# Two streams' memory reads in turn on two column groups of TensorE, and the first transfers of the stage in another order

## The chip, the cores and the metric

One core of one Trainium2 chip. The metric is the device time of one launch in microseconds, here the median of three runs. TensorE's granted clock is one of two levels, 1.2 or 2.4 GHz; the profile writes it as 0.5 or 1.0.

## What is computed

The whole program is one step of a two-layer streaming encoder: an S5 layer, an mLSTM layer with a matrix memory, a gated convolution FFN behind each. There are 1024 new prompt tokens and 8 running streams of 16 tokens. The change touches only the mLSTM part of the 8 running streams. Cut to that, for each of 4 heads and each of 8 streams:

```
num   = einsum('bqsh,bshd->bqhd', sc, vc) + a * einsum('bqhk,bhvk->bqhv', qc, C)   # reads of the old memory C
C_new = decay * C + einsum('blh,blhv,blhk->bhvk', wg, vc, kc)                      # update of it
```

C is a float32 matrix of 512 by 512 for each head and stream, 1 MB. So 32 memories are loaded from HBM, read, updated and stored back.

## The kernel before

`mlstm_streams` has three blocks; at the end of each, all engines meet in a barrier, and GpSimd comes to the barrier only when the transfers that it issued have landed.

The **first block** goes over the 4 heads. SyncE (the queue SP) loads `nrow` (the normalisers), `row` (gate rows, four transfers), and for each head `xc` and `xm` (semaphore `x_in`); `c_load` loads the memories of the first three streams into the three buffers `craw`. TensorE transposes `nrow`, then projects each head's q, k and v (`cell.project`, L2488 and L2491) and multiplies q by k (L2949). ScalarE and VectorE copy the results, scale them and split v and k into a rounded head and a rest; `write(h)` stores the four parts to DRAM. From the third head on GpSimd calls `stack_load`: twelve transfers per head bring the parts back, stacked on 16 partitions each, into `v3` and `k3`. Heads 0 and 1 are loaded here, heads 2 and 3 in the second block, each once an earlier head is done. A head's project waits for the work of the head before it, so the heads follow each other as a chain.

The **second block** is a loop over the 32 memories, `order` listing (head, stream). For one memory TensorE does 16 transposes into four PSUM banks (L3073; ScalarE copies each bank into the strips `cts`, L3087), two updates (L3055: rank-48 outer products into banks 5 and 7, each in two alternate uses), two reads, two updates, two reads (L3061). VectorE adds each update to the decayed memory and writes the strips `cnew` (L3099), of which there are two sets. When VectorE is through with a memory, SP issues the load of the memory three further on, then two stores of `cnew`. VectorE's next use of the same `cnew` set waits for these stores (`c_kept`).

A read multiplies a stationary tile of 32 columns (`qz`) by 512 columns of transposed memory, in float32, which the trace shows as two matmul instructions. The 32 columns are a pair of neighbouring streams with the other stream's half set to zero; the result goes to PSUM partitions 32·pair to 32·pair+31 of one bank:

```
ins = pe.matmul(num[32 * pair:32 * pair + 32, :], qz[h][k][:, 64 * pair + 32 * r:64 * pair + 32 * r + 32],
                strip(cts + k), start=False, stop=(k == HT - 1), skip_group_check=True)
```

The **third block** finishes normaliser, norm and output of the streams and is not touched.

The S5 layer has an instruction that the prediction uses for comparison, L411 in `s5`: float32, stationary tiles of 64 columns, 144 moving columns, results for g = 0 and g = 1 in turn on PSUM partitions 0 to 63 and 64 to 127 of one bank.

```
for o in range(2):
    for g in range(2):
        m = pe.matmul(bank[4 + p % 4][STATE * g:STATE * g + STATE, CW * o:CW * o + CW],
                      wt[p // BATCH][:, o, p % BATCH, STATE * g:STATE * g + STATE], uT[:, 2 * p + g, :],
```

Of the kernel before, what the change touches and what calls it, by code (L numbers as in the profile page):

```python
# [45 lines left out]
INNER, HEADS, DH = 2048, 4, 512  # L46
IT = INNER // P
HT = DH // P
# [3 lines left out]
PCH = SEQ // P  # L52
# [2469 lines left out]
def flat(a):  # L2522
    return a[:, :, :].rearrange("p a b -> p (a b)")
# [323 lines left out]
def mlstm_streams(env, cell, par, rows_d, cols, tri_s, last_s, member, xm_d, xc_d, sz_d, C_in, n_in, hs, c_out, n_out):  # L2847

    nc, bank = env.nc, env.bank
# [4 lines left out]
    with ExitStack() as scope:  # L2854
# [11 lines left out]

        two_strips = lambda n: hs[:, n // 2, 0:2 * DH].rearrange("p (a b) -> p a b", a=2)
        v3, k3 = ([env.sb(f"{n}{k}", [P, HEADS, DH], F32R) for k in range(2)] for n in ("v3", "k3"))
        cnew, cts = [8, 12], 16
        craw = [[strip(4 * b + t) for t in range(HT)] for b in range(2)] + [[flat(t) for t in (*cell.xc, *cell.xm)]]  # L2870
        homes = [[strip(28), strip(29)], [strip(30), strip(31)], [flat(t) for t in tiles[0:2]], [flat(t) for t in cell.qa]]
        qz = [[home[k // 2][:, 256 * (k % 2):256 * (k % 2) + 256] for k in range(HT)] for home in homes]
# [6 lines left out]
        def over(eng, sem, value):  # L2879

            if value > 0:
                eng.wait_ge(sem, value)

        x_in = [env.sem(f"x_in{k}") for k in range(2)]
        (nrow_in, n_turned, projected, qk, kwd, row_in, exp_in, exped, masked, lasts, summed, d_bank4, scored,
         weighted, v_headed, v_split, k_split, cleared, v_copied, k_headed) = (env.sem(n) for n in (
# [22 lines left out]
        with nc.Block() as block:  # L2909
            @block.sync  # L2910
            def _(sp):
                def write(h):
                    sp.wait_ge(v_split, h + 1)
                    sp.wait_ge(k_split, h + 1)
                    for dst, src in ((v_parts[h, 0], v_head), (v_parts[h, 1], v_rest), (k_parts[h, 0], k_head), (k_parts[h, 1], k_rest)):
                        sp.dma_start(dst, src[h % 2]).then_inc(wrote[h % 2], 16)

                sp.dma_start(nrow[:, :], n_in[0].rearrange("s h k -> (s h) k")).then_inc(nrow_in, 16)
                for h in range(HEADS):
                    sp.dma_start(row[:, h, :], rows_d[h, PCH].rearrange("k t -> (k t)").partition_broadcast(P)).then_inc(row_in, 16)  # L2920
                for h in range(HEADS):
                    over(sp, projected, h - 1)
                    for dst, src in ((cell.xc, xc_d), (cell.xm, xm_d)):
                        sp.dma_start(dst[h % 2][:, :, :], src.rearrange("k p t -> p k t")[:, HT * h:HT * h + HT, last]).then_inc(
                            x_in[h % 2], 16)
                    if h >= 1:
                        c_load(sp, h - 1, h - 1, 0) if h < 3 else None
                    if h >= 2:
                        write(h - 2)
                write(2)  # L2930
                write(3)
                sp.wait_ge(projected, HEADS)
                c_load(sp, 2, 2, 0)

            @block.tensor
            def _(pe):
                pe.wait_ge(nrow_in, 16)
                for k in range(HT):
                    ins = pe.transpose(bank[6][:, SR * k:SR * k + SR], nrow[:, P * k:P * k + P], env.ident[0:SR, 0:SR])
                ins.then_inc(n_turned, 1)  # L2940
                for h in range(HEADS):
                    pe.wait_ge(x_in[h % 2], 32 * (h // 2 + 1))
                    for sem in (qk, kwd, v_copied):
                        over(pe, sem, h)
                    cell.project(pe, env, h, h % 2).then_inc(projected, 1)
                    pe.wait_ge(qk, h + 1)
                    over(pe, weighted, h)
                    for t in range(HT):
                        ins = pe.matmul(bank[5][:, 0:P], cell.k[h % 2][:, t, :], cell.q[h % 2][:, t, :], start=(t == 0), stop=(t == HT - 1))  # L2949
                    ins.then_inc(scored, 1)  # L2950

            @block.scalar
            def _(act):
# [34 lines left out]

            @block.vector
            def _(dve):  # L2990
                dve.wait_ge(n_turned, 1)
                dve.tensor_copy(nt[:, :, :].rearrange("p k r -> p (k r)"), bank[6][:, 0:HT * SR])
                for h in range(HEADS):
                    y = h % 2
                    if h == 0:
                        dve.wait_ge(row_in, 16 * HEADS)
                    over(dve, masked, h - 1)
                    over(dve, lasts, h - 1)
                    dve.tensor_scalar(cell.e[y][:, :], row[:, h, 0:P], cols[:, PCH, 0, h:h + 1], 0.0, ALU.add,
                                      ALU.min).then_inc(exp_in, 1)  # L3000
                    dve.wait_ge(projected, h + 1)
                    dve.tensor_copy(flat(v[h]), bank[3][:, :]).then_inc(v_copied, 1)
                    dve.wait_ge(qk, h + 1)
                    dve.wait_ge(cleared, HT * h + HT)
                    for k in range(HT):
                        ins = dve.tensor_tensor(own_q(qz[h][k]), in_pairs(cell.q[y][:, k, :]), in_pairs(adec[:, h, :]), ALU.mult)
                    ins.then_inc(d_bank4, 1)
                    dve.wait_ge(v_headed, h + 1)
                    dve.tensor_tensor(as_r(v_rest[y]), flat(v[h]), v_head[y], ALU.subtract).then_inc(v_split, 1)

                    dve.wait_ge(lasts, h + 1)
                    dve.tensor_reduce(wg[:, h:h + 1], cell.h[y][:, 0, :], AX.X, ALU.add).then_inc(summed, 1)
                    dve.wait_ge(masked, h + 1)
                    dve.wait_ge(scored, h + 1)
                    dve.tensor_tensor(sc[h][:, :], cell.em[y][:, :], bank[5][:, 0:P], ALU.mult).then_inc(weighted, 1)
                    dve.wait_ge(k_headed, h + 1)
                    dve.tensor_tensor(as_r(k_rest[y]), flat(kw[h]), k_head[y], ALU.subtract).then_inc(k_split, 1)

        turned, copied, added, updated, inter, kept = (env.sem(n) for n in (
            "turned", "copied", "added", "updated", "inter", "kept"))  # L3020
        c_kept = [env.sem(f"c_kept{k}") for k in range(2)]
        order = [(h, s) for h in range(HEADS) for s in range(STREAMS)]

        with nc.Block() as block:
            @block.gpsimd
# [19 lines left out]

            @block.tensor
            def _(pe):
                for i, (h, s) in enumerate(order):
                    pair, r, p, num = s // 2, s % 2, i % 2, bank[4 + 2 * (h % 2)]

                    def updates(t0):
                        for t in (t0, t0 + 1):
                            over(pe, updated, HT * i + t - 1)
                            row = slice(64 * r, 64 * r + S3)
                            pe.matmul(bank[5 + 2 * (t % 2)][:, :], v3[h % 2][row, pair, P * t:P * t + P],  # L3055
                                      k3[h % 2][row, pair, :], start=True, stop=True).then_inc(added, 1)

                    def reads(k0):
                        for k in (k0, k0 + 1):
                            pe.wait_ge(copied, HT * i + k + 1)  # L3060
                            ins = pe.matmul(num[32 * pair:32 * pair + 32, :], qz[h][k][:, 64 * pair + 32 * r:64 * pair + 32 * r + 32],  # L3061
                                            strip(cts + k), start=False, stop=(k == HT - 1), skip_group_check=True)
                        return ins

                    if s == 0:
                        over(pe, kept, h - 1)
                        pe.matmul(num[:, :], sc[h][:, :], flat(v[h]), start=True, stop=False, skip_group_check=True)
                        pe.wait_ge(stacked[h % 2], 192 * (h // 2 + 1))
                    pe.wait_ge(c_in[i % 3], (32 if i % 3 < 2 else 64) * (i // 3 + 1))
                    for k in range(HT):  # L3070
# [1 line left out]
                        for t in range(HT):  # L3072
                            ins = pe.transpose(bank[k][:, P * t:P * t + P], craw[i % 3][t][:, P * k:P * k + P], env.ident[:, :])  # L3073
                        ins.then_inc(turned, 1)
                    updates(0)
                    reads(0)
                    updates(2)
                    reads(2).then_inc(inter, 1)

            @block.scalar  # L3080
            def _(act):
                for i, (h, s) in enumerate(order):
                    for k in range(HT):
                        act.wait_ge(turned, HT * i + k + 1)
                        if k == 0:
                            over(act, inter, i)
                        act.activation(strip(cts + k), bank[k][:, :], ACT.Copy).then_inc(copied, 1)  # L3087
                    if s == STREAMS - 1:
                        act.wait_ge(inter, i + 1)
                        act.activation(flat(inter_t[h]), bank[4 + 2 * (h % 2)][:, :], ACT.Copy).then_inc(kept, 1)  # L3090

            @block.vector
# [399 lines left out]
```

## Time and profile before

| | us |
|---|---|
| median of three runs (3980.96 to 3985.39) | 3983.93 |
| profiled execution: time | 3980.57 |
| its span | 3978.9 |
| TensorE busy in the span | 3531.2 (89%) |
| streams' first block, from its start to the end of its barrier | 1994.6 to 2058.7 |
| loop over the memories, from the second memory on | 2068.7 to 2293.2 |

The profile covers 3978.9 us, 1.7 less than the execution's own time. In the rows, an engine's busy time and what ended its idle time are those of one stretch; a row of matmuls counts instructions, two for each float32 read. Starts are microseconds from the span's start.

### The profile page before, as it was taken

To read this page: it belongs to the slowest core of one execution; us is meant where nothing else is said; L and a number is where in the kernel's file an instruction comes from. 1 tells how busy PE (TensorE), PEld (TensorE's weight loads), DVE (VectorE), ACT (ScalarE), POOL (GpSimd) and SP (SyncE) were. 2 spreads that over 40 slices of the span, in tenths; PEclk is the share of its full clock that TensorE was granted. 3 is DMA by queue.
4 is the path that set the end of the run, shared out by engine and by line. 5 is a ranking of instruction groups with operands and counts; after the bars stand their busy time and mean duration, and the time that the engine had idled before them with its cause. 6 is when DMAs were issued, how large, how long until landed. Compare 5 with 4: busy or idle time off the path is not lost. (4 is left out here: it accounts for less than half of the span.)

```text
span 3978.9 us, 53719 instructions
## 1 busy us (share of the span) xinstructions
PE 3531.2 (89%) x20489; PEld 3262.5 (82%) x20489; DVE 1909.4 (48%) x2968; ACT 1137.0 (29%) x1865; POOL 489.9 (12%) x729
## 2 busy tenths in 40 slices
PE   4549989999999989999459969997995999999997
PEld 4439889999999978999334458887995999999996
DVE  8923445445445562222523346664655454454455
ACT  5223343332233232222123212222113423322321
POOL 2240111010010010000021023222000100000000
PEclk7679999999999999999779979998997999999998
DMA  3554421111111222222179832222103111111112
GB/s 77 141 111 140 127 85 48 43 43 43 38 43 43 74 86 103 99 99 103 27 194 306 293 94 75 83 75 73 43 25 118 38 43 43 43 43 40 41 42 100
DMA packets 365214, 337.09 MB, mean 85 GB/s; under 512 B 42182, under 2 KB 292742, under 8 KB 364866
## 3 DMA queue, kind: packets, MB, share of 16 engines
q1 hardware_dynamic: 345332, 289.11, 23.8%
q0 software_dynamic: 12496, 37.61, 3.5%
q10 hardware_dynamic: 7176, 7.35, 0.6%
q8 instruction: 158, 2.59, 0.3%
q14 instruction: 52, 0.43, 0.0%
HBM read 231.12 MB, written 100.53 MB: 83 GB/s over the span
## 5 line engine op out<-in xcount | busy, mean ns | idle before, releaser
L1579 PE MATMUL pair<-x_head,w_head 128*128 128x384 f32 x1488 | 508.6, 342 | 66.4 <-DVE w_rest L840 38.4
L840 DVE TENSOR_TENSOR w_rest<-w_raw,w_head 128x1024 fp32r<-128x1024 f32 x228 | 282.0, 1237 | 469.0 <-ACT w_head L836 468.9
L1579 PE MATMUL pair<-x_rest,w_head 128*128 128x384 f32 x1488 | 505.5, 340 | 0.0
L1579 PE MATMUL pair<-x_head,w_rest 128*128 128x384 f32 x1488 | 505.1, 339 | 0.0
L836 ACT ACTIVATE w_head<-w_raw 128x1024 fp32r<-128x1024 f32 x228 | 242.6, 1064 | 742.6 <-PE pair L856 194.6
L1238 PE MATMUL pair<-x_head,w_head 128*128 128x384 f32 x1056 | 354.2, 335 | 10.2 <-DVE w_rest L840 7.6
L1238 PE MATMUL pair<-x_rest,w_head 128*128 128x384 f32 x1056 | 353.6, 335 | 0.0
L1238 PE MATMUL pair<-x_head,w_rest 128*128 128x384 f32 x1056 | 353.6, 335 | 0.0
L1579 PEld LDWEIGHTS pair<-x_head,w_head 128*128 128x128 f32 x1488 | 285.8, 192 | 72.3 <-issue 63.0
L1579 PEld LDWEIGHTS pair<-x_rest,w_head 128*128 128x128 f32 x1488 | 285.8, 192 | 0.0
L1579 PEld LDWEIGHTS pair<-x_head,w_rest 128*128 128x128 f32 x1488 | 285.6, 192 | 0.0
L1328 DVE SCALAR_TENSOR_TENSOR cv<-u,par,cv 128x1024 f32<-128x1024 f32 x88 | 112.8, 1282 | 358.3 <-ACT u L1294 358.3
L1847 DVE SCALAR_TENSOR_TENSOR cv<-u,par,cv 128x1024 f32<-128x1024 f32 x88 | 112.8, 1282 | 341.6 <-ACT u L1788 341.6
L1238 PEld LDWEIGHTS pair<-x_head,w_head 128*128 128x128 f32 x1056 | 198.9, 188 | 11.2 <-issue 8.5
L1238 PEld LDWEIGHTS pair<-x_rest,w_head 128*128 128x128 f32 x1056 | 199.0, 188 | 0.0
L1238 PEld LDWEIGHTS pair<-x_head,w_rest 128*128 128x128 f32 x1056 | 198.9, 188 | 0.0
L1749 PE MATMUL pair<-a_head,w_head 128*128 128x384 f32 x528 | 178.9, 339 | 2.1 <-DVE f L1878 0.9
L1259 PE MATMUL pair<-a_head,w_head 128*128 128x384 f32 x528 | 179.3, 340 | 1.5 <-DVE f L1355 0.4
L1289 ACT ACTIVATE cv<-pair,par 128x384 f32<-128x384 f32 x132 | 88.5, 671 | 315.2 <-PE pair L1238 304.2
L1259 PE MATMUL pair<-a_rest,w_head 128*128 128x384 f32 x528 | 177.5, 336 | 0.0
L1259 PE MATMUL pair<-a_head,w_rest 128*128 128x384 f32 x528 | 177.5, 336 | 0.0
L1749 PE MATMUL pair<-a_head,w_rest 128*128 128x384 f32 x528 | 176.7, 335 | 0.0
(501 smaller groups left out, 6919.7 us busy)
## 6 DMA issues: line engine op xcount, KB each, us to landing
w_raw<-in_ffn_w_up_dram SPq DMA_DIRECT2D x88, 512.0 KB, 3.8
out_dram<-hs SPq DMA_DIRECT2D x64, 512.0 KB, 7.0
w_raw<-in_s_w_glu_dram SPq DMA_DIRECT2D x48, 512.0 KB, 4.1
w_raw<-in_ffn_w_down_dram SPq DMA_DIRECT2D x44, 512.0 KB, 3.7
hs<-in_state_mlstm_C_dram SPq DMA_DIRECT2D x44, 512.0 KB, 5.9
w_raw<-in_mlstm_w_up_dram SPq DMA_DIRECT2D x32, 512.0 KB, 4.3
f<-in_state_mlstm_C_dram SPq DMA_DIRECT2D x40, 256.0 KB
xm_d<-xm SPq DMA_DIRECT2D x16, 576.0 KB, 3.9
```

Source lines behind the costliest of these rows:

```text
L836: act.activation(self.head[slot][:, :], self.raw[slot][:, :], ACT.Copy).then_inc(self.rounded, 1)
L840: dve.tensor_tensor(self.rest[slot][:, :], self.raw[slot][:, :], self.head[slot][:, :].bitcast(F32), ALU.subtract).then_inc(self.split, 1)
L1238: m = pe.matmul(banks[k % 2][c][:, 0:TB], lhs[k % 2][:, P * i:P * i + P], rhs[:, i, TB * c:TB * c + TB], start=(i == 0 and q == 0), stop=( ...
L1259: ins = pe.matmul(banks[m % 2][c][:, 0:TB], lhs[m // 4][:, cols], rhs[s][:, k, TB * c:TB * c + TB], start=(k == 0 and q == 0), stop=(k == ...
L1289: act.activation(cv[g][:, TB * c:TB * c + TB], bk[c][:, 0:TB], ACT.Identity, scale=at(par, t, TAP + H, TAP + H + 1), bias=at(par, t, BIAS, ...
L1328: ins = dve.scalar_tensor_tensor(out=cp, in0=up[:, j:j + SEQ], scalar=tw, in1=cp, op0=ALU.mult, op1=ALU.add)
L1579: m = pe.matmul(out[:, 0:TB], lhs[slot][:, P * k:P * k + P], rhs[:, k, TB * c:TB * c + TB], start=(k == 0 and q == 0), stop=(k == KD - 1 a ...
L1749: ins = pe.matmul(out[:, 0:TB], lhs[m // 4][:, cols], rhs[s][:, k, TB * c:TB * c + TB], start=(k == 0 and q == 0), stop=(k == 1 and q == 2))
L1847: ins = dve.scalar_tensor_tensor(out=cp, in0=up[:, j:j + SEQ], scalar=tw, in1=cp, op0=ALU.mult, op1=ALU.add)
```

## The change

In the second block the order of streams within a head becomes 0, 2, 4, 6, 1, 3, 5, 7, so that two successive memories belong to different pairs and so to different groups of 32 output partitions. The transposed memory gets a second home: `cts[0]` are the old strips, `cts[1]` the tiles `t1` and `t2`, which the first block uses as `v_rest` and `k_head`, so that ScalarE waits once for the stores of these. TensorE does no reads after an even memory; after an odd one it does the reads of both, k by k, one of each in turn. The four updates of a memory come in one go: behind the transposes of an even memory, behind the reads of an odd one. ScalarE may overwrite `cts` when the pair's reads are through.

In the first block SP issues the transfers of the first head first, then `row`, then `nrow`; the load of memory 1 moves behind `write(1)`, that of memory 2 ahead of `write(3)`. The transposes of `nrow` and VectorE's copy of them move to the block's end.

```diff
-        cnew, cts = [8, 12], 16
+        cnew = [8, 12]
+        cts = [[strip(16 + k) for k in range(HT)], [flat(t) for t in (*cell.t1, *cell.t2)]]
+        order = [(h, s) for h in range(HEADS) for s in (0, 2, 4, 6, 1, 3, 5, 7)]
...
-                sp.dma_start(nrow[:, :], n_in[0].rearrange("s h k -> (s h) k")).then_inc(nrow_in, 16)
-                for h in range(HEADS):
-                    sp.dma_start(row[:, h, :], ...).then_inc(row_in, 16)
-                for h in range(HEADS):
+                def inputs(h):
                     over(sp, projected, h - 1)
                     for dst, src in ((cell.xc, xc_d), (cell.xm, xm_d)):
...
+                inputs(0)
+                for h in range(HEADS):
+                    sp.dma_start(row[:, h, :], ...).then_inc(row_in, 16)
+                sp.dma_start(nrow[:, :], n_in[0].rearrange("s h k -> (s h) k")).then_inc(nrow_in, 16)
+                inputs(1)
+                c_load(sp, 0, order[0][1], 0)
+                inputs(2)
+                write(0)
+                inputs(3)
+                write(1)
+                c_load(sp, 1, order[1][1], 0)
                 write(2)
+                sp.wait_ge(projected, HEADS)
+                c_load(sp, 2, order[2][1], 0)
                 write(3)
-                sp.wait_ge(projected, HEADS)
-                c_load(sp, 2, 2, 0)
...
+                def reads(i, k):
+                    h, s = order[i]
+                    pair, r = s // 2, s % 2
+                    pe.wait_ge(copied, HT * i + k + 1)
+                    return pe.matmul(bank[4 + 2 * (h % 2)][32 * pair:32 * pair + 32, :], qz[h][k][:, 64 * pair + 32 * r:64 * pair + 32 * r + 32],
+                                     cts[i % 2][k], start=False, stop=(k == HT - 1), skip_group_check=True)
...
-                    updates(0)
-                    reads(0)
-                    updates(2)
-                    reads(2).then_inc(inter, 1)
+                    if i % 2 == 0:
+                        updates()
+                    else:
+                        for k in range(HT):
+                            for j in (i - 1, i):
+                                ins = reads(j, k)
+                        ins.then_inc(inter, 1)
+                        updates()
...
+                    if i == 1:
+                        act.wait_ge(wrote[0], 128)
+                        act.wait_ge(wrote[1], 128)
...
-                            over(act, inter, i)
-                        act.activation(strip(cts + k), bank[k][:, :], ACT.Copy).then_inc(copied, 1)
+                            over(act, inter, i // 2)
+                        act.activation(cts[i % 2][k], bank[k][:, :], ACT.Copy).then_inc(copied, 1)
```

TensorE, the first two memories of the second block, before. `k_354,v_352` are `k3` and `v3`; a row counts source matmuls.

```order
L3073 MATMUL pair<-ident,hs 128x128 x16
L3055 MATMUL pair<-k_354,v_352 128x512 x2
L3061 MATMUL pair<-hs 32x512 x2
L3055 MATMUL pair<-k_354,v_352 128x512 x2
L3061 MATMUL pair<-hs 32x512 x2
L3073 MATMUL pair<-ident,hs 128x128 x16
L3055 MATMUL pair<-k_354,v_352 128x512 x2
L3061 MATMUL pair<-hs 32x512 x2
L3055 MATMUL pair<-k_354,v_352 128x512 x2
L3061 MATMUL pair<-hs 32x512 x2
```

The same two memories in the changed kernel; reads from `hs` are of the even memory, those from `c_t` of the odd one.

```order
L3079 MATMUL pair<-ident,hs 128x128 x16
L3068 MATMUL pair<-k_354,v_352 128x512 x4
L3079 MATMUL pair<-ident,hs 128x128 x16
L3058 MATMUL pair<-hs 32x512
L3058 MATMUL pair<-c_t_335,hs 32x512
L3058 MATMUL pair<-hs 32x512
L3058 MATMUL pair<-c_t_336,hs 32x512
L3058 MATMUL pair<-hs 32x512
L3058 MATMUL pair<-c_t_337,hs 32x512
L3058 MATMUL pair<-hs 32x512
L3058 MATMUL pair<-c_t_338,hs 32x512
L3068 MATMUL pair<-k_354,v_352 128x512 x4
```

All eight reads stand together now, with the two sources in turn, and each memory's four updates are in one piece.

SP, the start of the first block, before:

```order
L2918 DMA nrow<-in_state_mlstm_n_dram 32x512
L2920 DMA row<-rows_d 128x256 x4
L2924 DMA f<-xc_d 128x4x128
L2924 DMA f<-xm_d 128x4x128
L2924 DMA f<-xc_d 128x4x128
L2924 DMA f<-xm_d 128x4x128
L2896 DMA hs<-in_state_mlstm_C_dram 128x2x512 x2
```

and in the changed kernel:

```order
L2923 DMA f<-xc_d 128x4x128
L2923 DMA f<-xm_d 128x4x128
L2926 DMA row<-rows_d 128x256 x4
L2929 DMA nrow<-in_state_mlstm_n_dram 32x512
L2923 DMA f<-xc_d 128x4x128
L2923 DMA f<-xm_d 128x4x128
L2898 DMA hs<-in_state_mlstm_C_dram 128x2x512 x2
```

The first head's inputs stand ahead of five transfers that they stood behind.

## Rows read from the trace of the kernel before

**Rows 1.** Busy by stretch: length, PE, PEld, DVE, ACT, POOL, granted clock, DMA share, GB/s.

```profile
1994.60:2058.70 64.10, 23.84 (x164) 22.27 (x165) 15.71 (x41) 12.48 (x24) 21.44 (x48) 0.71 0.87 206
2068.70:2293.20 224.50, 220.66 (x875) 96.77 (x874) 86.97 (x124) 66.06 (x127) 11.98 (x24) 0.98 0.91 295
2134.00:2142.00 8.00, 8.00 (x31) 3.07 (x29) 2.81 (x4) 2.07 (x4) 0.00 (x0) 0.94 1.03 397
```

**Rows 2.** Groups by line, 2068.7 to 2293.2.

```profile
L3061 PE MATMUL pair<-hs 128*32 128x512 f32 x185 | 90.4, 611 | 0.0
L3055 PE MATMUL pair<-k,v 48*128 48x512 f32 x124 | 46.2, 448 | 3.8 <-DVE hs L3099 3.7
```

**Rows 3.** Timeline of one memory of the loop: start, duration, instruction.

```profile
2089.38 1.97 PE L3073 MATMUL pair<-ident,hs 128*128 128x128 f32 x16
2090.07 2.07 ACT L3087 ACTIVATE hs<-pair 128x512 f32<-128x512 f32 x4 [4.82 <-PE pair L3073]
2091.28 0.73 PE L3055 MATMUL pair<-k,v 48*128 48x512 f32 x2
2091.88 1.41 DVE L3099 SCALAR_TENSOR_TENSOR hs<-hs,row,pair 128x512 f32<-128x512 f32 x2 [3.05 <-PE pair L3055]
2091.94 1.90 PE L3061 MATMUL pair<-hs 128*32 128x512 f32 x4
2093.77 0.73 PE L3055 MATMUL pair<-k,v 48*128 48x512 f32 x2
2094.43 1.90 PE L3061 MATMUL pair<-hs 128*32 128x512 f32 x4
2096.27 0.33 PE L3073 MATMUL pair<-ident,f 128*128 128x128 f32 x1
```

**Rows 4.** Timeline of the tenth memory, where VectorE waited for stores.

```profile
2129.70 2.74 DVE L3099 SCALAR_TENSOR_TENSOR hs<-hs,row,pair 128x512 f32<-128x512 f32 x4 [5.54 <-DMA out_dram<-hs]
2130.50 0.49 PE L3055 MATMUL pair<-k,v 48*128 48x512 f32 x1 [1.33 <-DVE hs L3099]
...
2131.59 3.56 PE L3061 MATMUL pair<-hs 128*32 128x512 f32 x4
```

**Rows 5.** Line L411: count, shortest, median, longest ns, first and last start.

```profile
L411 PE MATMUL pair<-uT,wt x256: 286/286/337, 80.4 to 96.7; 128*64 128x144 f32 x128
```

**Rows 6.** Waits in the loop: sum, times, longest.

```profile
DVE hs L3099 <- DMA out_dram<-hs: 35.5, 7, 6.1
```

**Rows 7.** Line L3041, the stores of memories.

```profile
DMA to landing us min/median/max: 2.9/7.0/12.8
```

**Rows 8.** Timeline of the first block.

```profile
1994.67 0.34 SPq L2918 DMA_DIRECT2D nrow<-in_state_mlstm_n_dram  x1
1995.06 4.09 SPq L2920 DMA_DIRECT2D row<-rows_d  x4
1999.19 0.43 SPq L2924 DMA_DIRECT2D f<-xc_d  x1
1999.67 0.51 SPq L2924 DMA_DIRECT2D f<-xm_d  x1
2003.10 0.29 DVE L2999 TENSOR_SCALAR c_e<-row,cols 128x128 f32<-128x128 f32 x1 [3.78 <-DMA row<-rows_d]
2004.89 3.78 PE L2488 MATMUL pair<-f,bd 128*128 128x128 f32 x16 [5.91 <-DMA f<-xm_d]
2022.52 3.55 PE L2488 MATMUL pair<-f,bd 128*128 128x128 f32 x16 [1.76 <-ACT f L2968]
2031.04 3.14 POOL L2906 DMA_DIRECT2D v<-v_parts  x6
2031.95 2.02 PE L2488 MATMUL pair<-f,bd 128*128 128x128 f32 x16 [1.76 <-ACT hs L2968]
2041.98 3.00 POOL L2906 DMA_DIRECT2D k<-k_parts  x6
2058.73 2.05 PE L3067 MATMUL pair<-f,c_sc 128*128 128x512 f32 x2 [20.63 <-PEq L2909]
```

More of the change, by code:

```diff
@@ L2916, in write @@
                         sp.dma_start(dst, src[h % 2]).then_inc(wrote[h % 2], 16)
-                sp.dma_start(nrow[:, :], n_in[0].rearrange("s h k -> (s h) k")).then_inc(nrow_in, 16)
-                for h in range(HEADS):
-                    sp.dma_start(row[:, h, :], rows_d[h, PCH].rearrange("k t -> (k t)").partition_broadcast(P)).then_inc(row_in, 16)
-                for h in range(HEADS):
+                def inputs(h):
                     over(sp, projected, h - 1)
@@ L2925, in _ @@
                             x_in[h % 2], 16)
[L2926 to L2929, printed above, removed]
+                inputs(0)
+                for h in range(HEADS):
+                    sp.dma_start(row[:, h, :], rows_d[h, PCH].rearrange("k t -> (k t)").partition_broadcast(P)).then_inc(row_in, 16)
+                sp.dma_start(nrow[:, :], n_in[0].rearrange("s h k -> (s h) k")).then_inc(nrow_in, 16)
[6 more added lines that the diff above has]
+                c_load(sp, 1, order[1][1], 0)
                 write(2)
+                sp.wait_ge(projected, HEADS)
+                c_load(sp, 2, order[2][1], 0)
                 write(3)
-                sp.wait_ge(projected, HEADS)
-                c_load(sp, 2, 2, 0)
             @block.tensor
             def _(pe):
[L2937 to L2940, printed above, removed]
                 for h in range(HEADS):
@@ L2950, in _ @@
                     ins.then_inc(scored, 1)
+                pe.wait_ge(nrow_in, 16)
+                for k in range(HT):
+                    ins = pe.transpose(bank[6][:, SR * k:SR * k + SR], nrow[:, P * k:P * k + P], env.ident[0:SR, 0:SR])
+                ins.then_inc(n_turned, 1)
             @block.scalar
@@ L2990, in _ @@
             def _(dve):
-                dve.wait_ge(n_turned, 1)
-                dve.tensor_copy(nt[:, :, :].rearrange("p k r -> p (k r)"), bank[6][:, 0:HT * SR])
                 for h in range(HEADS):
@@ L3017, in _ @@
                     dve.tensor_tensor(as_r(k_rest[y]), flat(kw[h]), k_head[y], ALU.subtract).then_inc(k_split, 1)
+                dve.wait_ge(n_turned, 1)
+                dve.tensor_copy(nt[:, :, :].rearrange("p k r -> p (k r)"), bank[6][:, 0:HT * SR])
         turned, copied, added, updated, inter, kept = (env.sem(n) for n in (
@@ L3021, in mlstm_streams @@
         c_kept = [env.sem(f"c_kept{k}") for k in range(2)]
-        order = [(h, s) for h in range(HEADS) for s in range(STREAMS)]
         with nc.Block() as block:
@@ L3047, in _, with updates @@
             def _(pe):
+                def reads(i, k):
[4 more added lines that the diff above has]
+                                     cts[i % 2][k], start=False, stop=(k == HT - 1), skip_group_check=True)
                 for i, (h, s) in enumerate(order):
-                    pair, r, p, num = s // 2, s % 2, i % 2, bank[4 + 2 * (h % 2)]
-                    def updates(t0):
-                        for t in (t0, t0 + 1):
+                    pair, r = s // 2, s % 2
+                    def updates():
+                        for t in range(HT):
                             over(pe, updated, HT * i + t - 1)
@@ L3056, in updates @@
                                       k3[h % 2][row, pair, :], start=True, stop=True).then_inc(added, 1)
[L3058 to L3063, printed above, removed]
                     if s == 0:
                         over(pe, kept, h - 1)
-                        pe.matmul(num[:, :], sc[h][:, :], flat(v[h]), start=True, stop=False, skip_group_check=True)
+                        pe.matmul(bank[4 + 2 * (h % 2)][:, :], sc[h][:, :], flat(v[h]), start=True, stop=False, skip_group_check=True)
                         pe.wait_ge(stacked[h % 2], 192 * (h // 2 + 1))
@@ L3074, in _ @@
                         ins.then_inc(turned, 1)
-                    updates(0)
-                    reads(0)
-                    updates(2)
-                    reads(2).then_inc(inter, 1)
+                    if i % 2 == 0:
+                        updates()
+                    else:
+                        for k in range(HT):
+                            for j in (i - 1, i):
+                                ins = reads(j, k)
+                        ins.then_inc(inter, 1)
+                        updates()
             @block.scalar
@@ L3085, in _ @@
                         if k == 0:
-                            over(act, inter, i)
-                        act.activation(strip(cts + k), bank[k][:, :], ACT.Copy).then_inc(copied, 1)
+                            over(act, inter, i // 2)
+                        act.activation(cts[i % 2][k], bank[k][:, :], ACT.Copy).then_inc(copied, 1)
                     if s == STREAMS - 1:
-                        act.wait_ge(inter, i + 1)
+                        act.wait_ge(inter, (i + 1) // 2)
                         act.activation(flat(inter_t[h]), bank[4 + 2 * (h % 2)][:, :], ACT.Copy).then_inc(kept, 1)
```

## The prediction, made before the changed kernel ran

> **What bounds the kernel now.** I read the busy times by stretch first. The first block takes 64.1 us with TensorE busy for only 23.8 of them; the loop takes 224.5 us with TensorE busy for 220.7 [rows 1]. So the first block is a chain of waits, and the loop is bound by TensorE. But in the loop the DMA engines are also at a share of 0.91, with 295 GB/s: whatever frees TensorE has little room before the transfers bound.
>
> The groups by line say what fills TensorE: 249 instructions of reads at L3061 and 124 updates at L3055 (L3061 stands in two groups; the one shown has 185 of them) [rows 2]. The timeline of one memory gives the spacing, which matters more than the modelled durations. Transposes start at 2089.38, updates at 2091.28, reads at 2091.94, updates at 2093.77, reads at 2094.43, the next transposes at 2096.27 [rows 3]. So 1.90 us of transposes, 2 × 0.66 of updates, 1.83 + 1.84 of reads: 6.89 in all. A burst of four read instructions lasts 1.90, a single one 0.61 [rows 2], so from one start to the next it is (1.90 − 0.61)/3 = 0.43 us. Behind the last of a burst it is 1.83 − 3 × 0.43, about 0.53, since other work follows.
>
> VectorE waited seven times for a store, 35.5 us in all [rows 6], of which some 3 us each time is the gap that it has anyway before a memory [rows 3, 4]. Those waits lie around the `stack_load` transfers for heads 2 and 3.
>
> **Change, part 1: the reads.** For two memories there are 16 read instructions, 16 × 0.43 = 6.9 us if they run one behind the other. Do two groups of output partitions run at once? L411 answers for groups of 64: its 256 instructions stream 144 columns each, and by the step of L3061 one of them should take 0.43 × 144/512 = 0.121 us, 31 us in all. They start within 96.7 − 80.4 = 16.3 us [rows 5], a factor of 0.53, and they alternate in the same way (two instructions to one group, two to the other) into one bank. I take the same for groups of 32. In program order, with each group doing one instruction at a time, the second instruction of one group runs with the first of the other, so 16 instructions need 9 steps: 8 × 0.43 + 0.53 = 3.97 us. By the bare factor it would be 16 × 0.43 × 0.53 + 0.1 = 3.7 us, the lower bound; the upper is 6.98. I take 3.97, since L411 has the same order of instructions.
>
> The Trainium skill (TensorE: Matmul & The Clock Gate, Part 3) states the same: matmuls on different column tiles overlap, and three tiles with 512 columns gave 2.38 times the speed. By that page the reads of a pair would be about 3.5 us and the time some 7 us lower than mine. This case's trace agrees, by the 16.3 us against 31.
>
> **Part 2: the updates in one go.** This edit costs. The third update needs the bank that VectorE empties first, the fourth the next. VectorE starts 0.60 us behind the first update [rows 3]. Where it was late by itself, the third update started 0.80 behind VectorE's start (2130.50 − 2129.70), and the reads another 1.09 later (2131.59 − 2130.50) [rows 4]. So four updates hold TensorE for 0.60 + 0.80 + 1.09 = 2.49 us where two halves took 1.32. Before, the first two reads covered VectorE; now nothing does.
>
> **The sum for two memories.** Transposes 2 × 1.90, updates 2 × 2.49, reads 3.97: 12.75 us. Before 2 × 6.89 = 13.78. That is 1.03 us saved for each of 16 pairs, 16.5 us: the reads save 3.37 (2 × 3.67 against 3.97), and 2.34 of it goes back into the waits for VectorE. ScalarE's copies are no wait: they end 2.76 us behind a memory's first transpose (2090.07 + 2.07 − 2089.38) [rows 3], and the pair's reads of the last quarter start 1.90 + 6 × 0.43 = 4.5 behind it. Its one wait for `wrote` is over long before. At the loop's end the updates come last now: VectorE is done 0.60 + 2.74 − 2.49 = 0.85 us behind the end of TensorE's share [rows 4]. Before, it was done 0.49 ahead of it (its last pair 0.60 + 1.41 = 2.01 behind updates that start 2.50 before the end). So the last stores start 1.3 us later against the sum: −1.3.
>
> **Part 3: do the transfers keep up?** A memory in and one out is 2.1 MB; at 12.75 us for two, 329 GB/s. Before it was 305. The eight us from 2134 to 2142, where work had piled up, moved 397 GB/s [rows 1], so the rate itself is there. But the finishing times of the updates become uneven: the even memory's updates end about 1.90 + 2.49 = 4.4 us behind the odd one's, the odd one's 8.4 behind those. An even memory's load and store therefore queue behind the odd one's. At 397 GB/s each burst takes 5.3 us. The odd burst, with the shortest landing of 2.9 us [rows 7] as its start-up, is done at 8.2 and the even one at 13.5, which is 9.1 behind the even updates' end. VectorE wants that buffer 12.75 − 2.74 = 10.0 us behind it. 0.9 us to spare: it holds, barely. The `stack_load`s of heads 2 and 3 come on top in both kernels. They stall the loop before, and with less slack they stall it longer: I charge 2 us for each of the two, −4.
>
> The Trainium skill (DMA: Bandwidth & Descriptors, Where 436 GB/s comes from) speaks against the change: it puts the HBM limit of a core near 358 GB/s for such transfers. By that page a pair would need 11.7 us and the stalls would grow. The trace does not bear it out as a limit of short stretches, with 397 over eight us.
>
> Loop: 16.5 − 1.3 − 4 = 11.2 us.
>
> **Part 4: the first block.** The first head's inputs are issued at 1999.19 and 1999.67, behind `nrow` and four `row`s which take SP 4.5 us to issue; TensorE starts on them at 2004.89 [rows 8]. Now they are issued at 1994.67 and 1995.15. With the same 5.2 us to land, project starts 4.5 us earlier; `row` no longer shares the engines, so it may be 5 to 6. I take 5. VectorE needs all `row`s before it copies v. They are issued 0.9 us later and so come at 2004.0 instead of 2003.10, while the projection ends some 5.6 us behind its start, near 2005.5: no wait. The chain then carries the 5 us on through four heads, to GpSimd's stack loads (2031.04 and up to 2044.98), and the end at 2058.7 lies behind them, in the landing of GpSimd's last transfers [rows 8]. SP's moved steps: the loads of memories 1 and 2 are needed only in the loop, `write(0)` now waits behind nothing later than it needs, and the load of memory 1 (1 MB, 2.6 us at 397 GB/s) is through before GpSimd starts. The load of memory 2 ahead of `write(3)` costs it nothing, since it is issued while the k of head 3 is still being split. The transposes of `nrow` and their copy at the block's end cost nothing: GpSimd comes to the barrier 13 us later. If one of the projections meets the low clock it takes 3.55 us instead of 2.02 [rows 8]; this may fall either way, ±1.5.
>
> **Total.** 11.2 + 5 = 16.2 us. The profiled execution took 3980.57, so 3964.4; the median of three is 3.4 us above it, so I predict 3967.
>
> **Rivals.**
>
> *The transfers bound the loop.* For: the share of 0.91, 0.9 us to spare, stores that took up to 12.8 us to land [rows 7], and VectorE's waits for them in the kernel before. Against: 397 GB/s where work was queued. If the engines give only the 305 to 318 GB/s that the bursts average now, a pair takes 13.2 to 13.8 us, the loop gains 0 to 9 us less the 5.3 for its end and the stalls, and the first block's 5 us come to that: 3975 to 3984, the middle 3979.
>
> *The groups of 32 don't run side by side.* The mechanism that ends on the other side. The reads then take 6.98 us, the updates' waits stay, and a pair takes 3.80 + 4.98 + 6.98 = 15.76 us, 1.98 more than before: +31.7 for 16 pairs, less 5 from the first block, so 3984 + 31.7 − 5 + 1.3 = 4012. It decides from the point where a pair's reads take 5.0 us or more instead of 3.97: there the whole change is worth nothing. For: no row shows tiles of 32 columns in turn. Against: L411 with tiles of 64.
>
> *The first block gives nothing.* The order of transfers does what it says, but the stack loads, 24 transfers onto 16 partitions each, might be paced by something that doesn't move, or a low clock eats it. The loop alone gives 3984 − 11.2 = 3973.
>
> *The updates wait less than I charge,* with the reads at the lower bound: up to 8 us better, 3959.
>
> **How the numbers follow.** The forecast 0.48, the better case 0.12, first block without effect 0.12, transfers bound 0.21, no side-by-side 0.07. A measurement of this kernel can tell about 0.2%, 8 us. The forecast, the better case and the first block's case are faster by more than that; the transfers' case is half and half. So faster 0.81, same 0.12, slower 0.07. The range reaches from the better case to the middle of the transfers' case: 3957 to 3979. The 4012 stays out, and the worst of the transfers' case.
>
> **What the changed profile would show.** The 16 read instructions of a pair within 3.7 to 4.1 us (side by side), and not 7. The third update of a memory waiting for VectorE, some 1.1 us each time. Transposes of every second memory 12.75 us apart. VectorE's waits for the stores about as now, with more near the stack loads; if these waits come with every even memory, the transfers bound. The first project near 2000 instead of 2004.89, and the barrier's end near 2053.7. Everything behind the streams unchanged but shifted. I am wrong if read starts stay 0.43 us apart, or if a pair takes 13.3 us or more with VectorE waiting for `out_dram`.

## The result, and the profile after

The changed kernel is slower: 3994.24 us median of 9 runs (3989.53 to 4003.3) against 3985.39 (3980.46 to 3994.91, 9 runs) before. The ratio is 1.0024, interval 1.0013 to 1.0034, so it is 5 to 14 us slower. The forecast was 3967, faster.

The profiled execution has a span of 3992.5 us. First the busy times: the first block, the loop from its first product to the start of VectorE's last update, and two pairs of memories of the loop. The columns are those of [rows 1]. The loop there began with the second memory; the line by itself below is the whole loop of the kernel before, from the same points.

```profile
1991.20:2052.60 61.40, 24.02 (x164) 22.55 (x164) 15.60 (x41) 12.47 (x24) 21.52 (x48) 0.72 0.88 215
2052.60:2300.90 248.30, 216.68 (x904) 121.02 (x904) 87.51 (x127) 75.00 (x132) 12.08 (x24) 0.81 0.82 267
2243.50:2255.80 12.30, 10.63 (x58) 5.58 (x56) 4.64 (x7) 4.13 (x8) 0.00 (x0) 1.00 0.91 298
2132.50:2150.30 17.80, 15.93 (x58) 9.29 (x57) 5.48 (x8) 4.78 (x8) 0.00 (x0) 0.64 0.91 300
```

```profile
2058.70:2291.80 233.10, 229.24 (x902) 101.62 (x903) 88.99 (x127) 68.34 (x131) 11.98 (x24) 0.98 0.88 284
```

The first block is 2.7 us shorter (64.1 before), the loop 15.2 us longer: 248.3 us against 233.1. The clock column points to the reason. TensorE's granted clock is 0.81 on average in the loop, where it was 0.98. A pair that has the full clock throughout takes 12.3 us; the pair at 2132.5, at 0.64 on average, takes 17.8, with the same instructions.

Now the instructions of the full-clock pair, from the timeline of TensorE; the dots stand for the remaining reads:

```profile
2243.52 1.91 PE L3079 MATMUL pair<-ident,hs 128*128 128x128 f32 x16
2245.36 0.73 PE L3068 MATMUL pair<-k,v 48*128 48x512 f32 x2
2246.76 0.50 PE L3068 MATMUL pair<-k,v 48*128 48x512 f32 x1 [0.67 <-DVE hs L3112]
2247.42 0.50 PE L3068 MATMUL pair<-k,v 48*128 48x512 f32 x1 [0.16 <-DVE hs L3112]
2247.85 1.97 PE L3079 MATMUL pair<-ident,hs 128*128 128x128 f32 x16
2249.75 0.62 PE L3058 MATMUL pair<-hs,f 128*32 128x512 f32 x1
2249.76 0.62 PE L3058 MATMUL pair<-c_t,f 128*32 128x512 f32 x1
2250.20 0.59 PE L3058 MATMUL pair<-hs,f 128*32 128x512 f32 x1
2250.21 0.59 PE L3058 MATMUL pair<-c_t,f 128*32 128x512 f32 x1
...
2253.31 0.73 PE L3068 MATMUL pair<-k,v 48*128 48x512 f32 x2
```

Reads of the two memories (`hs` and `c_t`) start 0.01 us apart, and the next two about 0.45 later. From the first read to the updates it is 3.56 us for 16 instructions: the groups of 32 partitions do run side by side, in 8 steps. Each memory's third update starts 1.40 us behind the first, with TensorE idle for 0.67 of it and for 0.16 more before the fourth.

The pair at 2132.5, same view:

```profile
2132.48 3.67 PE L3079 MATMUL pair<-ident,hs 128*128 128x128 f32 x16
2136.09 1.22 PE L3068 MATMUL pair<-k,v 48*128 48x512 f32 x2
2138.34 1.45 PE L3068 MATMUL pair<-k,v 48*128 48x512 f32 x2 [1.04 <-DVE hs L3112]
2139.72 3.67 PE L3079 MATMUL pair<-ident,f 128*128 128x128 f32 x16
2143.33 1.06 PE L3058 MATMUL pair<-hs 128*32 128x512 f32 x1
2143.33 1.06 PE L3058 MATMUL pair<-c_t,hs 128*32 128x512 f32 x1
...
2145.54 0.59 PE L3058 MATMUL pair<-hs 128*32 128x512 f32 x1
```

At 1.2 GHz both sets of transposes take 3.6 us instead of 1.9, and the first reads are 0.85 apart; the clock comes back in the middle of the reads. Of the 15 distances from one pair's transposes to the next pair's, one is 12.3 us, the others are 13.9 to 18.1; three of them also hold the products of a new head, about 1 us.

The first block's timeline, to be set beside [rows 8]:

```profile
1991.26 0.41 SPq L2923 DMA_DIRECT2D f<-xc_d  x1
1991.73 2.39 SPq L2923 DMA_DIRECT2D f<-xm_d  x1
1997.31 3.78 PE L2488 MATMUL pair<-f,bd 128*128 128x128 f32 x16 [13.62 <-DMA f<-xm_d]
1999.88 0.29 DVE L3004 TENSOR_SCALAR c_e<-row,cols 128x128 f32<-128x128 f32 x1 [14.98 <-DMA row<-rows_d]
2034.83 3.05 POOL L2908 DMA_DIRECT2D k<-k_parts  x6
2052.66 2.05 PE L3073 MATMUL pair<-f,c_sc 128*128 128x512 f32 x2 [21.34 <-PEq L2911]
```

The first projection starts 6.05 us behind SP's first transfer of the block, where it was 10.22 (2004.89 − 1994.67). VectorE starts on `row` at 1999.88, long before TensorE's projection is through, so `row` comes in time.

### The profile page after: what moved, and what is told of

Read it like the earlier page. It is cut to its first block and busy times, and to the rows that moved or that the text cites. A ratio compares the mean times of both kernels' runs of the same rounds, so it can differ in the third digit from the quotient of the medians.

```text
span 3992.5 us, 53719 instructions
## 1 busy us (share of the span) xinstructions
PE 3519.8 (88%) x20489; PEld 3285.7 (82%) x20489; DVE 1906.7 (48%) x2968; ACT 1142.5 (29%) x1865; POOL 489.6 (12%) x729
```

## The experiments

My theory after these rows (A): the idle time inside the updates, 0.83 us in each memory and so 1.7 us in a pair of 12.3, lowers the clock. Rival B: the reads side by side halve the time in reads, and that alone lowers it. Rival C: the loop is held up by transfers, not by the clock. Beside each time stand two readings of its profile: the loop, measured as above, and the mean granted clock in it. The kernel before has 233.1 us and 0.98, the changed one 248.3 and 0.81. Ratios are to the kernel before, which was timed anew beside each group of experiments (medians 3985.39 for the names with e1, 3982.99 for e2, 3981.81 for e3). Kernels of different groups are therefore compared by their ratios; 0.1% is 4 us.

**e1_front**: the loop of before behind the changed first block.

```diff
-                sp.dma_start(nrow[:, :], n_in[0].rearrange("s h k -> (s h) k")).then_inc(nrow_in, 16)
...
+                inputs(0)
...
```

> The changed first block (transfers reordered, nrow's transposes last) with the loop of before. It isolates part 4. If the shorter first block is worth what the two traces show (61.4 us instead of 64.1 from barrier to barrier), the kernel is 2.5 to 3 us faster than before and the loop keeps its 233 us. Rival: what the first block gains is given back in the loop or behind it, then the time is that of before; the clock in the loop stays at 0.98 either way.

Measured: 3976.49 us, ratio 0.9976 (0.9966 to 0.9985), 6 to 13 us faster. Loop 236.1 us, clock 0.98. The expectation was 2.5 to 3 us. From the last copy of the gates (L2049, an instruction ahead of the block, the same in all kernels) to the loop's first product it is 137.8 us, 142.4 before. Over all ten profiles with the new block this stretch has a mean of 137.7 us (135.7 to 139.7), over the three with the old one 141.9 (141.0 to 142.4). So the first block gives 4.2 us. The timed gain is larger by some us, for which no row of the loop or block speaks. Outside the part that changed, the profiles of all kernels differ too: the last copy of the gates starts at 1908.4 to 1917.2, and the stretch behind the loop takes 1686.2 to 1692.1.

**e1_samegroup**: the changed kernel, streams in natural order, so nothing runs side by side.

```diff
-        order = [(h, s) for h in range(HEADS) for s in (0, 2, 4, 6, 1, 3, 5, 7)]
+        order = [(h, s) for h in range(HEADS) for s in range(STREAMS)]
```

> The changed kernel with the streams in their natural order, so that the two memories of a pair write to the same group of 32 partitions and nothing runs side by side; the updates stay in one go. Theory A (the waits inside the updates lower the clock): four waits of 1.1 us in every 15.8 us instead of every 12.3, so the clock falls less often but still falls, mean 0.85 to 0.95, a pair 16 to 17 us, 30 to 45 us slower than before. Theory B (the reads side by side leave too little busy time, waits or not): with 6.9 us of reads in a row the clock holds at 0.98 and a pair takes 15.8 us, 28 us slower. Either way a pair's reads take 7 us and not 3.5.

Measured: 4035.11 us, ratio 1.0123 (1.0099 to 1.0146). Busy times of its loop:

```profile
2055.20:2346.70 291.50, 261.20 (x904) 127.62 (x904) 87.38 (x128) 73.79 (x132) 12.03 (x24) 0.88 0.70 227
```

The clock, 0.88, falls without anything running side by side: against B, and as A had it. The time is 50 us above the kernel before (39 to 58), more than the 30 to 45 of A: the pairs take 15.7 us at best, most of them 17.4 to 19. And the side-by-side reads are worth 43 us of the loop (291.5 against 248.3) even at the poor clock.

**e1_fill**: three products more in TensorE's wait, in each memory but the first of a head; their results are not used.

```diff
+                            if t == 2 and s:
+                                over(pe, kept, h)
+                                for _ in range(3):
+                                    pe.matmul(bank[6 - 2 * (h % 2)][:, 0:P], env.ident[:, :], sc[h][:, :], start=True, stop=True,
+                                              skip_group_check=True)
                             over(pe, updated, HT * i + t - 1)
```

> The changed kernel with three extra 128-column float32 products of sc into an unused bank between the second and third update of each memory but the first of a head, 0.64 us of work where TensorE waits 0.7 us; nothing else changed, the extra results are not used. Theory A (idle time lowers the clock): the clock rises to 0.95 or more, a pair comes from 15.4 us on average to 12.5 to 13.2, the kernel 8 to 18 us faster than before. Theory B: the clock stays near 0.8 and the time near that of the changed kernel.

Measured: 3976.82 us, ratio 0.9979 (0.997 to 0.9989), by the ratios 18 us less than the changed kernel, and 9 us below the kernel before, with 168 more instructions. Busy times of its loop:

```profile
2052.80:2282.60 229.80, 210.93 (x1072) 122.80 (x1072) 88.61 (x128) 70.28 (x132) 11.99 (x24) 0.92 0.88 288
```

The clock is 0.92 and four pairs take 12.3 us. A's mark of 0.95 is not reached, and 229.8 us is more than 16 × 12.3 = 197 us. VectorE's waits for stores are 41.9 us now in ten waits, against 20.2 in four in the changed kernel (the second line):

```profile
DVE hs L3117 <- DMA out_dram<-hs: 41.9, 10, 7.5
```

```profile
DVE hs L3112 <- DMA out_dram<-hs: 20.2, 4, 9.0
```

As one cause is mended the other grows.

**e1_split**: the updates in halves, with other work between, and no extra work. `updates(i, t)` now issues updates t and t + 1 of memory i.

```diff
...
                     if i % 2 == 0:
-                        updates()
+                        updates(i, 0)
                     else:
+                        updates(i - 1, 2)
                         for k in range(HT):
                             for j in (i - 1, i):
                                 ins = reads(j, k)
+                            if k == 1:
+                                updates(i, 0)
                         ins.then_inc(inter, 1)
-                        updates()
+                        updates(i, 2)
```

> The changed kernel with the updates in halves again, spread so that other TensorE work covers VectorE: transposes, updates 1-2 of the even memory, transposes of the odd, updates 3-4 of the even, half of the pair's reads, updates 1-2 of the odd, the other reads, updates 3-4 of the odd. Reads still side by side. Theory A: no waits, so the clock holds at 0.95 or more, a pair would take 10.3 us of TensorE and is bounded by the transfers at 11 to 12.5 us; the loop comes to 190 to 215 us instead of 233, the kernel 18 to 40 us faster than before. But then TensorE waits for transfers, and those waits may lower the clock as well, which costs little as TensorE is not the bound. Theory B: transposes and updates alone lower the clock, mean 0.8, a pair 12.5 to 14 us, no more than 0 to 15 us faster than before.

Measured: 3966.5 us, ratio 0.9947 (0.9928 to 0.9966), 19 us below the kernel before. Loop 231.4 us, clock 0.86, and this wait:

```profile
DVE hs L3115 <- DMA out_dram<-hs: 87.5, 20, 9.8
```

Twenty waits of VectorE for stores, where [rows 6] has seven. TensorE has less to do, and the stores' way out holds up the loop: eight of 15 pairs take 13 to 15 us, though the fastest takes 11.2. TensorE is idle for 32 us of this loop too (231.4 − 198.96), 30.6 of it in waits for VectorE, which itself waits for these stores. That these waits lower the clock as those inside the updates did is my reading; nothing here separates it. The time is just inside the range that A gave (18 to 40 us faster). The loop and the clock are not: A wanted 190 to 215 us and 0.95.

**e2_split3**: the same with a third set of output strips, in tiles that are free in the loop. The edits of SP's stores and of VectorE's wait are left out below.

```diff
-        c_kept = [env.sem(f"c_kept{k}") for k in range(2)]
+        c_kept = [env.sem(f"c_kept{k}") for k in range(3)]
+        third = [flat(t) for t in (*cell.hn, *cell.sz)]
+        per = (32, 32, 64)
+        new = lambda i, t: strip(cnew[i % 3] + t) if i % 3 < 2 else third[t]
...
```

> The split order of updates and side-by-side reads, with a third set of output strips for the updated memories (the tiles hn and sz, free in the loop), so that VectorE waits for the stores of three memories back instead of two. If the round trip of a store through two sets is what bounds the split kernel (VectorE waited 20 times, 87.5 us), those waits fall to under 30 us, a pair comes from 14 us to 11 to 12, and the kernel is another 20 to 35 us faster than the split one, about 3935 to 3948. If the rate of the transfers itself is the bound (2.1 MB each at the 289 GB/s of the split loop), the waits only move to the loads and the time stays within 5 us of the split kernel's.

Measured: 3951.69 us, ratio 0.9926 (0.9909 to 0.9943): the fastest of all here, by the ratios 29 us below the kernel before and 39 below the changed one. Its loop and its waits for transfers:

```profile
2053.20:2259.50 206.30, 180.46 (x904) 98.67 (x904) 89.30 (x128) 70.75 (x132) 12.04 (x24) 0.91 0.94 321
```

```profile
PE pair L3086 <- DMA hs<-in_state_mlstm_C_dram: 16.1, 6, 8.1
PE pair L3086 <- DMA f<-in_state_mlstm_C_dram: 9.2, 4, 6.5
DVE hs L3124 <- DMA out_dram<-hs: 6.1, 2, 4.2
```

The waits for stores are down from 87.5 us to 6.1, and TensorE waits for loads instead. Undisturbed pairs take 10.1 us. The time came out 4 us above the expected range, and the third set gave less than the 20 to 35 us expected of it: the loop is 25.1 us shorter in one profile of each, but the ratios differ by 0.21%, 8 us, with overlapping intervals. With 321 GB/s in the loop the rate of the transfers was not what bound the split kernel at 286; the two sets were.

**e2_front3**: the loop of before, the new first block, three sets; the same edit as above.

> The first block as changed, the loop of before, with the third set of output strips. The loop of before lost some 8 us around the stack loads waiting for stores; if two sets are the reason, 4 to 8 us faster than the kernel with the changed first block alone, 3969 to 3973; if the stack loads take the engines whatever the buffers, within 3 us of it.

Measured: 3968.58 us, ratio 0.9966 (0.9954 to 0.9979). Loop 224.8 us, 11.3 less than in e1_front, clock 0.99, no wait for a store. By the ratios it is 4 us below e1_front, with overlapping intervals, so the times alone don't decide between the two expectations.

**e2_onego**: the kernel before, updates in one go.

```diff
                     updates(0)
-                    reads(0)
                     updates(2)
+                    reads(0)
                     reads(2).then_inc(inter, 1)
```

> The kernel before with one edit: the four updates of a memory in one go ahead of its four reads. No pairs, no side-by-side reads, old first block. The waits for VectorE cost 1.17 us a memory, 37 us in all at the full clock. Theory A (the waits lower the clock): the clock in the loop falls from 0.98 to 0.85 to 0.93 and the kernel is 45 to 60 us slower than before. Theory B (the reads side by side are needed for the clock to fall): clock 0.97 or more, 33 to 40 us slower.

Measured: 4033.98 us, ratio 1.0134 (1.0117 to 1.0151), 51 us slower. Its loop:

```profile
2050.70:2334.90 284.20, 256.53 (x897) 108.49 (x898) 87.04 (x127) 68.09 (x131) 11.94 (x24) 0.90 0.73 233
```

Two lines exchanged take the clock from 0.98 to 0.90. The full-clock pairs take 15.8 us, 2.0 more than before, which for 16 pairs is 32 us. The rest of the 51 goes with the clock, since VectorE's waits for stores are fewer here (11.3 us in two, 35.5 in [rows 6]). With no reads side by side, this decides between A and B: the waits are enough to lower the clock.

**e2_loop**: the loop's change behind the first block of before.

> The changed kernel with the first block of before, so the loop's change alone. If the two halves of the change add up, it is 18 us slower than before, 4003, with the loop at 245 to 250 us and its clock near 0.82. If the slow clock came from the state that the new first block leaves behind, the loop is at 233 us or less.

Measured: 3997.51 us, ratio 1.0043 (1.0026 to 1.0059), 15 us slower than before where 18 were expected. Loop 244.7 us, clock 0.83. The slow loop is its own doing, and the halves add up within their intervals: +0.43% and −0.24% against +0.24% for both.

**e3_changed3**: the changed kernel with three sets.

> The changed kernel with the third set of output strips, nothing else. If the clock is what costs the changed kernel its gain, the third set removes only VectorE's four waits for stores (20 us, of which some 10 hold anything up): 3 to 10 us faster than the changed kernel, 3984 to 3991, the clock in the loop still low for 70 to 100 us. If the stores were the hidden cause, the loop falls to 220 us or less and the kernel to 3965.

Measured: 3980.88 us, ratio 0.9993 (0.9982 to 1.0004). By the ratios that is 12 us below the changed kernel, where 3 to 10 were expected.

```profile
2054.90:2294.30 239.40, 210.94 (x904) 116.21 (x904) 87.20 (x127) 74.45 (x132) 11.93 (x24) 0.83 0.84 277
```

No wait of VectorE for a store is left, and the loop is 8.9 us shorter: the stores were a part. But the clock stays low and the loop is still longer than before, so transfers (C) are not the cause of the slower loop.

**e3_fill3**: the products and three sets.

> The changed kernel with both: the products in the wait between the second and third update (their results unused) and the third set of output strips. If the forecast's sum for a pair was right at the full clock, nearly all pairs take 12.3 us, the clock is low for less than 20 us of the loop, the loop takes 203 to 212 us and the kernel 3950 to 3962. If the products only mend part, or a pair's time is set by transfers, more than half of the pairs stay above 13 us.

Measured: 3957.44 us, ratio 0.9939 (0.9916 to 0.9962).

```profile
2055.40:2266.60 211.20, 202.72 (x1072) 117.02 (x1072) 88.95 (x128) 69.37 (x132) 11.94 (x24) 0.97 0.94 314
```

One filled wait of it, timeline of TensorE:

```profile
2243.60 0.73 PE L3080 MATMUL pair<-k,v 48*128 48x512 f32 x2
2244.26 0.94 PE L3076 MATMUL pair<-sc,ident 128*128 128x128 f32 x6
2245.12 1.04 PE L3080 MATMUL pair<-k,v 48*128 48x512 f32 x2
2246.09 1.97 PE L3091 MATMUL pair<-ident,f 128*128 128x128 f32 x16
```

The products (L3076) fill the wait without lengthening it: the four updates still hold TensorE for 2.49 us. The clock is 0.97. Nine of 15 pairs take 12.3 to 12.9 us, three more take 13.3 with a new head's products in them, and the last three 13.9 to 16.8. The loop and the time are in the ranges that A gave, and by the mean of 0.97 the low clock takes up some 13 us of the loop, under the 20 expected. The reads run side by side here as in the changed kernel, so B is out a second time.

**e3_fillturn**: six transposes in the place of the three products of e1_fill; the diff is to that kernel.

```diff
-                                for _ in range(3):
-                                    pe.matmul(bank[6 - 2 * (h % 2)][:, 0:P], env.ident[:, :], sc[h][:, :], start=True, stop=True,
-                                              skip_group_check=True)
+                                for _ in range(6):
+                                    pe.transpose(bank[6 - 2 * (h % 2)][:, 0:P], sc[h][:, :], env.ident[:, :])
```

> As the kernel with three products in the wait, but six transposes of sc instead (their results unused): by the spacing of 0.108 us the same 0.64 us of TensorE. If any instruction keeps the clock up, the time is that of the kernel with products, 3977, with the clock low for 30 to 45 us of the loop. If transposes count for less than products, the clock stays low for 70 to 100 us and the time is 3985 to 3997, near that of the changed kernel.

Measured: 3978.66 us, ratio 1.0 (0.9989 to 1.001).

```profile
2051.90:2285.90 234.00, 210.93 (x1072) 120.64 (x1072) 88.37 (x128) 70.65 (x132) 11.94 (x24) 0.92 0.88 283
```

In place of a wait, transposes hold the clock as well as products do. The time doesn't follow as closely: the ratio lies between that of the changed kernel (1.0024) and that of e1_fill (0.9979). VectorE waits longer for stores here, 56.9 us in 13 waits against 41.9 in ten; why is not shown.

## Why the prediction was wrong

**The reads (part 1) were right, and slightly better than forecast.** Groups of 32 run side by side. The two groups start together, so it is 8 steps and 3.56 us, not 9 and 3.97, and below the 3.7 that was to be the lower bound. The rival that they would not is out: 43 us of the loop lie between e1_samegroup and the changed kernel.

**The updates in one go (part 2): the direct price was right.** 2.49 us for four was forecast; in the full-clock pair it is 2.49 for the even memory (2247.85 − 2245.36). The sum for a pair, 12.75, came out as 12.3 where the clock was full and nothing else held the pair up; the 0.4 us between them is that of the reads.

**The step that failed is "The sum for two memories".** It priced every instruction by rows at the full clock, as if the 0.98 of [rows 1] belonged to the loop and not to the way its work is laid out. The waits that part 2 had just found cost twice: 1.17 us a memory directly, which was in the sum, and then the clock, 0.81 instead of 0.98, which was not. A pair that the sum put at 12.75 us took 13.9 to 18.1 in all but one case, and the loop 248.3 us where the forecast made 221.9. The prediction has a word on the clock for the first block alone. The clock and the stores act on each other, so their loops stand best in one table, us from first product to last update:

| | two sets of strips | three sets |
|---|---|---|
| changed kernel | 248.3 | 239.4 |
| with the wait filled | 229.8 | 211.2 |

Filling the wait takes 18.5 us from the changed loop and 28.2 from the one with three sets. The forecast was 233.1 − 11.2 = 221.9. So the clock is the largest part of the 26.4 us by which the loop exceeds it, and the third set's 8.9 us comes after it.

**Part 3, "it holds, barely", was off too.** With the wait filled the third set is worth 229.8 − 211.2 = 18.6 us of the loop, some of it by way of the clock (0.92 and 0.97), where the prediction charged 4 for the stores. 397 GB/s was a rate of eight us with work piled up; what decided was how soon the stores of two memories earlier landed. The prediction reckoned with the shortest landing, 2.9 us; in the changed kernel the median is 7.4 and the longest 14.5. In the changed kernel this was partly hidden, since a slow TensorE doesn't press on the stores: VectorE's waits for them are 20.2 us against 35.5 in [rows 6]. The rival "the transfers bound the loop" was thus a real second bound, in the buffers and not in the rate, but it doesn't explain the result: with three sets the changed loop still takes 239.4 us.

**The first block (part 4) was right in size:** 5 us forecast, 4.2 in the traces, and the first projection comes 4.2 us sooner (6.05 us against 10.22 behind the first transfer). Why the timed gain of that half is 9 us and not 4 stays open; its interval reaches down to 6. That the first block might give nothing is refuted. One slip of the total has no weight: 3980.57 − 16.2 + 3.4 is 3968 and not 3967.

**What is shown and what is not.** That the waits in the updates lower the clock is shown from three sides: brought into the kernel before (e2_onego), kept without side-by-side reads (e1_samegroup), and filled in the changed kernel (e1_fill, e3_fillturn, e3_fill3). How much idle time the clock bears isn't settled by these runs: in the kernel before, TensorE's idle time was a few us in 224 and the clock held. The sum of idle time alone doesn't settle it: it is 31.6 us at a clock of 0.81 in the changed loop, 32.4 at 0.86 in e1_split and 30.3 at 0.88 in e1_samegroup. Between the changed kernel and e1_samegroup only the reads side by side differ, with the same waits in every memory; whether the clock falls further because the waits stand closer together, or because of the reads themselves, is not shown. Nor was it tried to fill the waits for transfers.

## What to carry to other kernels

When an edit leaves idle time on TensorE, even 0.8 us in every six, ask for the granted clock of the new layout and price the pieces around the wait at both clocks. Running instructions side by side in column groups was a gain here even at the poor clock, but spend it on pieces laid between dependent steps, as the split order does, not on a block of its own with the waits put behind. And when the bound engine gets faster, count the buffers of the stores before the bandwidth: in the profiles a third set took 25 us from the split loop, 19 from the filled one, and 11 even from the old one. The timed gains by the ratios were 8, 16 and 4 us, and 12 in the changed kernel; only the 16 and the 12 are clear of the intervals.

## What the hardware showed that I had not expected

Instructions of two column groups start within 0.01 us of each other, also where each float32 product is two instructions: 16 read instructions in 3.56 us, against 7.3 before (four bursts of 1.83 to 1.84 us). A loop in which TensorE was busy for 216.7 of 248.3 us, 87%, had a mean granted clock of 0.81. Six float32 transposes in the wait, in 28 of 32 memories, held the clock at 0.92, the same as three float32 products.
